# Prompt attention of a hybrid decoder step: new places in the written-out order for the next head's transposes, the values' low part, the page sums and the maxima

## The chip, the cores and the metric

One Trainium2 chip, one of its cores. The kernel runs as one program on that core; the time is the device time of one execution in microseconds (us), the median of several runs.

## The reference

The whole kernel is one inference step of a hybrid decoder layer: a joint input projection, three token mixers, gates and an output projection. The change touches one stage, the forgetting attention over the prompt (2048 positions, 8 heads of 64), and a side calculation that shares its engines. Cut to what matters:

```python
def fox_attention(q, k, v, fq, fk, q_pos, k_pos):       # fq, fk: cumulated log forget values
    s = einsum('bqhd,bkhd->bhqk', q, k) * dh ** -0.5
    s = s + fq[..., :, None] - fk[..., None, :]
    s = where(k_pos <= q_pos, s, -inf)                   # causal
    return einsum('bhqk,bkhd->bqhd', softmax(s), v)

logf_all = concatenate([cache_logf[page_table], logf])   # sample group: 8 sequences x 8192 positions
cum_f = cumsum(logf_all, axis=1)
```

## The kernel before

Four stages run one after another: `project`, `attend_prompt`, `attend_sample` and the output. Barriers part them. Within a stage each engine has its own instruction stream, in an order fixed in the source, and streams meet at semaphores only.

`attend_prompt` works head by head. The 16 key tiles and 16 query tiles of 128 positions are cut into 4 groups of queries (`g`, 512 columns each); group g meets 4(g+1) key tiles (`j`). So a head has 4+8+12+16 = 40 steps, written (g, j) here, and the stage has 320. Products are made with float32r operands in two parts (high and low), so the scores take two matmuls of 512 columns (`kA`/`qA` hold the high part and the extra rows with decays and maxima, `kB`/`qB` the low parts and a second copy) and the weighing of the values takes three (`v_hi`·`p_hi`, `v_lo`·`p_hi`, `v_hi`·`p_lo`). The steps of the diagonal blocks are 512, 384, 256 and 128 columns wide.

The order is the function `all_steps`, which every engine walks through with its own class. For step s:

- `score(s)`: two matmuls on PE into one of 2 buffers `st_ps`; ACT takes the exponential into `probs` (L1429) and then casts the probabilities of step s-1 to `p_hi` (L1405).
- `past`: in every second head (a "pair"), sums over the cached log forget values for the later sample stage. DVE scans at (1, 0..7), PE has one small matmul at (2, 2), DVE makes `rest` at (2, 4) and three 128x1024 tensor operations (L1507, L1509, L1512) at (2, 5), (2, 6), (2, 7). GpSimd (POOL) gathers the values with an indirect DMA at (0, 0) and waits there until it has landed (L1373).
- `maximum`: row maxima that the softmax subtracts, one group ahead: PE multiplies `kA` and `qA` into one of 2 buffers `max_ps` (L1598), DVE reduces them (L1518). `negate` joins them (L1526), and `turn_max` brings them into row form: four PE transposes (L1583), one ACT copy into `qA` (L1423). `turn_max` is the last thing in the last step of a group, behind `weigh`.
- `split(h+1)` at (1, 4): DVE casts the next head's values to `v_hi` (L1455), POOL subtracts to get `v_lo` (L1378) for all 16 tiles.
- `decay(h+1)` at (2, 7), `turn(h+1, c)`: the next head's keys are transposed at (2, 8), (2, 9), (2, 10), (2, 11), its queries at (3, 1), (3, 3), (3, 5), (3, 7): four PE transposes each (L1571), then an ACT copy to `kA`/`qA` (L1416, L1418), then two DVE operations of 64x512 to `kB`/`qB` (L1475 and L1476, L1479 and L1480). Each turn of PE waits for the DVE part of the turn before, since they share a PSUM buffer.
- `weigh(s-4)`: POOL subtracts `p_lo` = `probs` - `p_hi` (L1392), PE has the three matmuls (L1635 to L1637). P is held in rings of 6.
- `turn_back`, 6 steps behind the last step of a group, that is at (1, 1), (1, 5), (2, 5), (3, 5): ACT copies the finished output out of PSUM (L1440), PE transposes it back (L1644), DVE normalizes it.

Before the first step, head 0 does all of its eight turns, its first maxima and `turn_max(0, 0)`. DVE clears the unused rows of `kA`, `qA` (`pad`, L1448) for head 0 there and for head 1 at (0, 0) and (0, 1) of head 0, and those of `o_sb` at (0, 2).

SP stores the page sums of a pair and loads heads 4 to 7, with waits on `turned`, `max_turned`, `vlo_ready` and `past_step`; after the last pair's page sums it starts the first loads of the sample stage.

Of the kernel before, what the change touches and what calls it, by code (L numbers as in the profile page):

```python
# [27 lines left out]
F32 = mybir.dt.float32  # L28
# [4 lines left out]
P = 128  # L33
# [1089 lines left out]
def attend_prompt(nc, arena, z, y_a, cache_logf, cache_k, page_table, decay_past):  # L1123
# [21 lines left out]
    LAG, BACK = 4, 2  # L1145
    P_RING = 6
    TURNS = 2 * GROUPS
    IN_GROUP = P // N_PAGES
    with ExitStack() as stack:
# [34 lines left out]
        consts, padded, filled = m.sem("consts"), m.sem("padded"), m.sem("filled")  # L1184
# [20 lines left out]
        FIRST_CONSTS, CONSTS = 4, 13  # L1205
# [21 lines left out]
        def all_steps(do):  # L1227

            do.split(0)
            do.decay(0)  # L1230
            for c in range(TURNS):
                do.turn(0, c)
# [4 lines left out]
            ends = {}  # L1237
            for s in range(STEPS + LAG + BACK):
                h, n = divmod(s, N_FIN)
                if s < STEPS:  # L1240
                    g, j = FIN[n]
                    last = h == HEADS - 1
                    do.score(s)
                    if h % 2 == 0:
                        do.past(h // 2, g, j)
# [7 lines left out]
                    if not last:  # L1253
                        if g == 1 and j == 4:
                            do.split(h + 1)
                        if g == 2 and j == 7:
                            do.decay(h + 1)
                        if g == 2 and j >= 8:
                            do.turn(h + 1, j - 8)
                        if g == 3 and j < 8 and j % 2 == 1:  # L1260
                            do.turn(h + 1, GROUPS + j // 2)
                        if g == 3 and 9 <= j < 9 + QG:
                            do.maximum(h + 1, MAX_UNITS[0][j - 9])
                            if j == 8 + QG:
                                do.negate(h + 1, 0)
                if LAG <= s < STEPS + LAG:
                    do.weigh(s - LAG)
                if s < STEPS:
                    if j == QG * (g + 1) - 1 and (g < GROUPS - 1 or not last):
                        do.turn_max(*((h, g + 1) if g < GROUPS - 1 else (h + 1, 0)))  # L1270
                done = s - LAG - BACK
                if done >= 0 and done % N_FIN + 1 in FIN_END:
                    do.turn_back(done // N_FIN, FIN_END.index(done % N_FIN + 1))

        class Part:

            past = decay = turn = turn_max = maximum = negate = score = weigh = turn_back = split = lambda self, *where: None

        @block.sync
        def _(sp):  # L1280
# [6 lines left out]
            def load(h):  # L1287
                if h >= 4:
                    sp.wait_ge(turned, (h - 1) * TURNS)
                    sp.wait_ge(max_turned, (h - 1) * GROUPS)  # L1290
                    sp.wait_ge(vlo_ready, h - 1)
# [9 lines left out]
            def begin_sample():  # L1301
# [4 lines left out]
                sp.wait_ge(vlo_ready, 2)  # L1306
# [34 lines left out]
        def _(pool):  # L1341
            def ones_of(k, q, done):
# [5 lines left out]
            ones_of(arena.k_first, arena.q_first, consts)  # L1348
            pool.memset(v_hi[:, :, :, HEAD_DIM:HEAD_DIM + 1].bitcast(F32), 1.0).then_inc(consts, 1)
# [18 lines left out]
            def gather(group):  # L1368
                pool.wait_ge(past_stored, 16)
                wait_from(pool, past_step, 3 * group)  # L1370
                pool.indirect_dma_start(lf[:], None, cache_logf.rearrange("l n k h -> (l n) (k h)"),
                                        bass.IndirectOffsetOnAxis(ap=page_of[:, group:group + 1], axis=0)).then_inc(gathered, 16)
                pool.wait_ge(gathered, 16 * (group + 1))  # L1373

            class GpSimdPart(Part):
                def split(self, h):
                    pool.wait_ge(vhi_ready, h + 1)
                    pool.tensor_tensor(v_lo[:, h % 2], v_of(h), v_hi[:, h % 2, :, 0:HEAD_DIM].bitcast(F32),  # L1378
                                       ALU.subtract).then_inc(vlo_ready, 1)
                    if h == 0:  # L1380
# [17 lines left out]
        def _(act):  # L1398
# [8 lines left out]
            class ScalarPart(Part):  # L1407
                def turn(self, h, c):
                    hh, at = h % 2, slice((c % GROUPS) * BLK, (c % GROUPS + 1) * BLK)
                    bank = c % 2 if h == 0 else 0  # L1410
                    if c == 0:
                        act.wait_ge(padded, 2 * min(h + 1, 2))
                        wait_from(act, st_done, (h - 1) * N_FIN)
                    act.wait_ge(turned, h * TURNS + (c + 1))
                    if c < GROUPS:
                        act.copy(kA[0:AUG, hh, at], t_ps[0:AUG, bank, :]).then_inc(k_high, 1)  # L1416
                    else:
                        act.mul(qA[0:AUG, hh, at], t_ps[0:AUG, bank, :], HEAD_DIM ** -0.5).then_inc(q_high, 1)  # L1418
# [16 lines left out]
                def turn_back(self, h, g):  # L1435
                    n = h * GROUPS + g
                    act.wait_ge(pv_done, h * N_FIN + FIN_END[g])
                    act.wait_ge(padded, 5)
# [6 lines left out]
        def _(dve):  # L1445

            def pad(x, hh):
                dve.memset(x[HEAD_DIM:P, hh].bitcast(F32), 0.0).then_inc(padded, 1)  # L1448

            class VectorPart(Part):  # L1450
                def split(self, h):
                    dve.wait_ge(v_loaded[slot_of(h)], loads_of(h))
                    wait_from(dve, pv_done, (h - 1) * N_FIN)
                    wait_from(dve, vlo_ready, h - 1)
                    dve.tensor_copy(v_hi[:, h % 2, :, 0:HEAD_DIM], v_of(h)).then_inc(vhi_ready, 1)  # L1455

                def decay(self, h):
# [4 lines left out]
                    if h == 0:  # L1462
                        pad(kA, 0)
                        pad(qA, 0)

                def turn(self, h, c):
                    hh, at = h % 2, slice((c % GROUPS) * BLK, (c % GROUPS + 1) * BLK)
                    bank = c % 2 if h == 0 else 0
                    if c == 0:
                        wait_from(dve, st_done, (h - 1) * N_FIN)  # L1470
                    dve.wait_ge(turned, h * TURNS + (c + 1))
                    src = t_ps[0:HEAD_DIM, bank, :]
                    if c < GROUPS:
                        dve.wait_ge(k_high, h * GROUPS + (c + 1))
                        dve.tensor_copy(kB[HEAD_DIM:P, hh, at], src)  # L1475
                        dve.tensor_tensor(kB[0:HEAD_DIM, hh, at], src, kA[0:HEAD_DIM, hh, at].bitcast(F32), ALU.subtract).then_inc(k_low, 1)  # L1476
                    else:
                        dve.wait_ge(q_high, h * GROUPS + (c - GROUPS + 1))
# [1259 lines left out]
```

## Time and profile before

| | |
|---|---|
| median of 3 runs | 3863.25 us (3862.15 to 3867.77) |
| the profiled execution: its time, its span | 3863.69 us, 3861.9 us |
| PE, DVE, ACT, POOL busy over the span | 94%, 48%, 47%, 37% |
| first and last score matmul of `attend_prompt` | 1815.2 us, 2466.7 us |
| granted TensorE clock over the span | 0.978 |

Matmuls are pipelined: a 512-column matmul is shown as some 0.4 us, while the next one starts 0.23 us after it. So the busy share of PE says little, and the waits and the start-to-start times say more. A wait is idle time after the modelled end of the matmul before it.

### The profile page before, as it was taken

To read this page: it belongs to the slowest core of one execution; us is meant where nothing else is said; L and a number is where in the kernel's file an instruction comes from. 1 tells how busy PE (TensorE), PEld (TensorE's weight loads), DVE (VectorE), ACT (ScalarE), POOL (GpSimd) and SP (SyncE) were. 2 spreads that over 40 slices of the span, in tenths; PEclk is the share of its full clock that TensorE was granted. 3 is DMA by queue.
4 is the path that set the end of the run, shared out by engine and by line. 5 is a ranking of instruction groups with operands and counts; after the bars stand their busy time and mean duration, and the time that the engine had idled before them with its cause. 6 is when DMAs were issued, how large, how long until landed. Compare 5 with 4: busy or idle time off the path is not lost. (4 is left out here: it accounts for less than half of the span.)

```text
span 3861.9 us, 54053 instructions
## 1 busy us (share of the span) xinstructions
PE 3622.5 (94%) x17931; PEld 2838.3 (73%) x17931; DVE 1861.5 (48%) x3114; ACT 1807.4 (47%) x3704; POOL 1414.2 (37%) x1063
## 2 busy tenths in 40 slices
PE   8999999999999999997787787899999999799999
PEld 7788888787788888885555555577777777588787
DVE  3234432323134533333545545488888888644432
ACT  4224433445224533442555565677777777411222
POOL 0011232220011232211555565577777777422200
PEclk9999999999999999997999999999999999899999
DMA  4234343333233344324001212299999999654422
GB/s 160 85 108 137 115 146 124 107 137 121 89 124 113 119 143 141 123 94 107 12 17 28 53 25 69 84 340 334 334 331 334 331 329 336 223 171 154 151 89 79
DMA packets 378554, 590.38 MB, mean 153 GB/s; under 512 B 93381, under 2 KB 114485, under 8 KB 378298
## 3 DMA queue, kind: packets, MB, share of 16 engines
q1 hardware_dynamic: 366146, 579.94, 44.4%
q10 hardware_dynamic: 11584, 5.13, 0.5%
q8 instruction: 145, 2.38, 0.3%
q0 software_dynamic: 576, 2.10, 0.2%
q14 instruction: 103, 0.84, 0.1%
HBM read 475.25 MB, written 111.83 MB: 152 GB/s over the span
## 5 line engine op out<-in xcount | busy, mean ns | idle before, releaser
L996 PE MATMUL prj_z_ps<-prj_w_hi,prj_h_hi 128*128 128x512 f32 x2312 | 923.9, 400 | 2.7 <-DVE prj_w_lo L792 2.7
L998 PE MATMUL prj_z_ps<-prj_w_hi,prj_h_lo 128*128 128x512 f32 x2312 | 902.4, 390 | 0.0
L997 PE MATMUL prj_z_ps<-prj_w_lo,prj_h_hi 128*128 128x512 f32 x2312 | 901.0, 390 | 0.0
L1874 POOL TENSOR_TENSOR sa_v_lo<-sa_v_raw,sa_v_hi 128x1024 fp32r<-128x1024 f32 x256 | 609.1, 2401 | 215.6 <-DVE sa_v_hi L2013 215.2
L998 PEld LDWEIGHTS prj_z_ps<-prj_w_hi,prj_h_lo 128*128 128x128 f32 x2312 | 434.2, 188 | 93.7
L996 PEld LDWEIGHTS prj_z_ps<-prj_w_hi,prj_h_hi 128*128 128x128 f32 x2312 | 435.3, 188 | 89.7 <-DVE prj_w_lo L792 5.4
L997 PEld LDWEIGHTS prj_z_ps<-prj_w_lo,prj_h_hi 128*128 128x128 f32 x2312 | 435.4, 188 | 84.7
L1392 POOL TENSOR_TENSOR pa_p_lo<-pa_probs,pa_p_hi 128x512 fp32r<-128x512 f32 (+1 forms) x320 | 362.0, 1147 | 230.0 <-ACT pa_p_hi L1405 207.0
L2007 DVE TENSOR_TENSOR sa_kT_lo<-sa_t_ps,sa_kT_hi 128x512 fp32r<-128x512 f32 x512 | 345.3, 686 | 136.3 <-ACT sa_kT_hi L1896 132.8
L424 POOL TENSOR_TENSOR prj_dist<-prj_cum 128x256 f32<-128x256 f32 x132 | 88.6, 671 | 796.3 <-DVE prj_cum L863 796.3
L1896 ACT CAST sa_kT_hi<-sa_t_ps 128x512 fp32r<-128x512 f32 x512 | 291.6, 590 | 125.5 <-PE sa_t_ps L2160 118.8
L2160 PE MATMUL sa_t_ps<-arena_ident,arena_k_raw 128*128 128x128 f32 x2048 | 300.9, 277 | 26.0 <-DVE sa_kT_lo L2007 18.1
L2160 PEld LDWEIGHTS sa_t_ps<-arena_ident,arena_k_raw 128*128 128x128 f32 x2048 | 241.8, 141 | 105.3 <-DVE sa_kT_lo L2007 33.2
L792 DVE TENSOR_TENSOR prj_w_lo<-arena_w_raw,prj_w_hi 128x512 fp32r<-128x512 f32 x274 | 193.2, 749 | 204.7 <-ACT prj_w_hi L660 203.8
L675 ACT ACTIVATE prj_z_sb<-prj_z_ps 128x512 f32<-128x512 f32 x153 | 91.2, 596 | 406.8 <-PE prj_z_ps L998 406.5
L1429 ACT ACTIVATE pa_probs<-pa_st_ps 128x512 f32<-128x512 f32 (+1 forms) x320 | 171.0, 534 | 227.7 <-PE pa_st_ps L1620 137.7
L672 ACT COPY prj_z_sb<-prj_z_ps 128x512 f32<-128x512 f32 (+2 forms) x124 | 72.2, 582 | 428.7 <-PE prj_z_ps L998 417.7
L1518 DVE TENSOR_REDUCE pa_part_max<-pa_max_ps 128x1 f32<-128x512 f32 (+2 forms) x320 | 183.4, 606 | 182.4 <-PE pa_max_ps L1598 145.3
L432 POOL TENSOR_TENSOR prj_kE<-prj_kT,prj_dec 128x256 f32<-128x256 f32 x115 | 93.0, 808 | 404.1 <-ACT prj_dec L711 385.1
L2223 PE MATMUL sa_o_ps<-sa_v_hi,sa_p_both 128*128 128x512 f32 x512 | 215.3, 420 | 8.4 <-POOL sa_v_lo L1874 5.3
L2166 PE MATMUL sa_s_ps<-sa_kT_hi,sa_q_both 128*128 128x512 f32 x512 | 212.6, 415 | 0.0
L2224 PE MATMUL sa_o_ps<-sa_v_lo,sa_p_both 128*64 128x512 f32 x512 | 204.0, 399 | 0.0
(327 smaller groups left out, 6447.2 us busy)
## 6 DMA issues: line engine op xcount, KB each, us to landing
arena_k_raw<-in_cache_k_dram SPq DMA_DIRECT2D x512, 256.0 KB, 4.0
sa_v_raw<-in_cache_v_dram SPq DMA_DIRECT2D x512, 256.0 KB, 4.3
arena_w_raw<-in_w_main_dram SPq DMA_DIRECT2D x272, 256.0 KB, 4.1
z_scratch<-prj_z_sb SPq DMA_DIRECT2D x272, 256.0 KB
arena_mg<-z_scratch SPq DMA_DIRECT2D x51, 512.0 KB, 4.2
arena_cu<-extp_scratch SPq DMA_DIRECT2D x48, 256.0 KB
arena_x_in<-in_x_all_dram SPq DMA_DIRECT2D x17, 512.0 KB, 3.7
prj_aux<-z_scratch SPq DMA_DIRECT2D x34, 256.0 KB, 2.8
```

The lines of the kernel that those rows point to most:

```text
L792: dve.tensor_tensor(w_lo[:, s % W_RING, 0:columns(s)], w_raw[:, s % RAW, 0:columns(s)], w_hi[:, s % W_RING, 0:columns(s)].bitcast(F32), AL ...
L996: pe.matmul(out, h_hi[:, slot_of(t), k], hi, start=(k == 0), stop=False)
L997: pe.matmul(out, h_hi[:, slot_of(t), k], lo, start=False, stop=False)
L998: mm = pe.matmul(out, h_lo[:, slot_of(t), k], hi, start=False, stop=(k == KC - 1))
L1392: pool.tensor_tensor(p_lo[:, s % P_RING, 0:w], probs[:, s % P_RING, 0:w], p_hi[:, s % P_RING, 0:w].bitcast(F32), ALU.subtract).then_inc(pl ...
L1874: pool.tensor_tensor(v_lo[:, w % 2, at], v_raw[:, w % RING, at], v_hi[:, w % 2, at].bitcast(F32), ALU.subtract).then_inc(vlo_ready, 1)
L1896: act.copy(kT_hi[:, g % 2, :, j * PAGE:(j + 1) * PAGE], heads_of(t_ps[:, j % 2])).then_inc(khi_ready, 1)
L2007: dve.tensor_tensor(kT_lo[:, g % 2, :, at], heads_of(t_ps[:, j % 2]), kT_hi[:, g % 2, :, at].bitcast(F32), ALU.subtract).then_inc(klo_read ...
L2160: mm = pe.transpose(t_ps[:, j % 2, pair * PAGE:(pair + 1) * PAGE], k_raw[:, g % RING, j, pair * P:(pair + 1) * P], ident[:])
L2166: pe.matmul(out, q, hi(pair), start=(pair == 0), stop=False, skip_group_check=True)
L2223: pe.matmul(out, p_both[:, slot, j], v_hi[:, slot, j], start=begin, stop=False, skip_group_check=True)
L2224: mm = pe.matmul(out[0:R], p_both[:, slot, j, 0:R], v_lo[:, slot, j], start=False, stop=end, skip_group_check=True)
```

## The change

The steps stay; what moves is where the side work stands in the order, with the semaphores split to suit.

- The next head's turns go key, query, key, query (`TURN_ORDER`), at (2, 4), (2, 6), (2, 8), (2, 10), (3, 0), (3, 2), (3, 4), (3, 6). `decay` goes to (2, 3).
- `turn_max` of a group stands ahead of `weigh`, at (0, 3), (1, 7), (2, 10), (3, 14).
- POOL's `v_lo` is made in two halves, at (2, 0) and (2, 2); the DVE cast stays at (1, 4).
- ACT's copy of a finished output (`take`) is one step earlier than the transposes.
- POOL no longer waits for the gather to land, it waits for the one before it at the next gather.
- The three page-sum operations of DVE go to (3, 9), (3, 11), (3, 13).
- Head 0 does four turns (groups 0 and 1) before its first step and the other four in (0, 0) to (0, 3); in its turns ACT writes the second copy for `kB`/`qB` (`first_b`), DVE only the low part. POOL clears `qA` for head 0; head 1's clearing goes to (2, 0) and (2, 2) of head 0, that of `o_sb` to (0, 3).

```diff
-    LAG, BACK = 4, 2
+    LAG, TAKE, BACK = 4, 1, 2
+    TURN_ORDER = [x for c in range(GROUPS) for x in ((0, c), (1, c))]
+    TURN_AT = {(2, 4): 0, (2, 6): 1, (2, 8): 2, (2, 10): 3, (3, 0): 4, (3, 2): 5, (3, 4): 6, (3, 6): 7}
+    MAX_TURN_AT = {(0, 3): 1, (1, 7): 2, (2, 10): 3, (3, 14): 0}
...
             do.split(0)
+            do.split_low(0, 0)
+            do.split_low(0, 1)
             do.decay(0)
-            for c in range(TURNS):
-                do.turn(0, c)
+            for n in range(4):
+                do.turn(0, n)
...
                     do.score(s)
+                    if h == 0 and g == 0:
+                        do.turn(0, 4 + j)
                     if h % 2 == 0:
                         do.past(h // 2, g, j)
...
-                        if g == 1 and j == 4:
+                        if (g, j) == (1, 4):
                             do.split(h + 1)
-                        if g == 2 and j == 7:
+                        if g == 2 and j in (0, 2):
+                            do.split_low(h + 1, j // 2)
+                        if (g, j) == (2, 3):
                             do.decay(h + 1)
-                        if g == 2 and j >= 8:
-                            do.turn(h + 1, j - 8)
-                        if g == 3 and j < 8 and j % 2 == 1:
-                            do.turn(h + 1, GROUPS + j // 2)
-                        if g == 3 and 9 <= j < 9 + QG:
-                            do.maximum(h + 1, MAX_UNITS[0][j - 9])
-                            if j == 8 + QG:
+                        if (g, j) in TURN_AT:
+                            do.turn(h + 1, TURN_AT[g, j])
+                        if g == 3 and 8 <= j < 8 + QG:
+                            do.maximum(h + 1, MAX_UNITS[0][j - 8])
+                            if j == 7 + QG:
                                 do.negate(h + 1, 0)
+                    if (g, j) in MAX_TURN_AT and (g < GROUPS - 1 or not last):
+                        do.turn_max(h if g < GROUPS - 1 else h + 1, MAX_TURN_AT[g, j])
                 if LAG <= s < STEPS + LAG:
                     do.weigh(s - LAG)
-                if s < STEPS:
-                    if j == QG * (g + 1) - 1 and (g < GROUPS - 1 or not last):
-                        do.turn_max(*((h, g + 1) if g < GROUPS - 1 else (h + 1, 0)))
-                done = s - LAG - BACK
-                if done >= 0 and done % N_FIN + 1 in FIN_END:
-                    do.turn_back(done // N_FIN, FIN_END.index(done % N_FIN + 1))
+                for do_it, done in ((do.take, s - LAG - TAKE), (do.turn_back, s - LAG - BACK)):
+                    if 0 <= done < STEPS and done % N_FIN + 1 in FIN_END:
+                        do_it(done // N_FIN, FIN_END.index(done % N_FIN + 1))
...
@@ gpsimd
+            pool.wait_ge(consts, FIRST_CONSTS)
+            pad(qA, 0)
+            pool.wait_ge(q_padded, 1)
...
                 wait_from(pool, past_step, 3 * group)
+                wait_from(pool, gathered, 16 * group)
                 pool.indirect_dma_start(lf[:], None, cache_logf.rearrange("l n k h -> (l n) (k h)"),
...
-                pool.wait_ge(gathered, 16 * (group + 1))
...
+                def split_low(self, h, half):
+                    tiles = slice(half * T // 2, (half + 1) * T // 2)
+                    if half == 0:
+                        pool.wait_ge(vhi_ready, h + 1)
...
@@ scalar, turn
                     act.wait_ge(turned, h * TURNS + (n + 1))
+                    if h == 0:
+                        act.mul((kB, qB)[is_q][B_HIGH[is_q], hh, at], t_ps[0:HEAD_DIM, bank, :],
+                                (1.0, HEAD_DIM ** -0.5)[is_q]).then_inc(first_b, 1)
...
@@ vector, past
-                    if j == 5:
+                    if (g, j) == (3, 9):
                         dve.wait_ge(rest_ready, pair + 1)
                         dve.tensor_tensor(log_rest, wide, cum[:], ALU.subtract).then_inc(past_step, 1)
-                    if j == 6:
+                    if (g, j) == (3, 11):
                         dve.tensor_tensor(d_hi[:], wide, cum[:], ALU.subtract).then_inc(past_step, 1)
-                    if j == 7:
+                    if (g, j) == (3, 13):
...
@@ tensor, score
-                        pe.wait_ge(k_low, (h + 1) * GROUPS)
-                        pe.wait_ge(q_low, (h + 1) * GROUPS)
+                        pe.wait_ge(q_low, h * GROUPS + (g + 1))
+                        if h == 0:
+                            pe.wait_ge(first_b, 2 * (g + 1))
+                    if j % QG == 0:
+                        pe.wait_ge(k_low, h * GROUPS + (j // QG + 1))
```

## Rows read from the trace of the kernel before

**Rows 1.** The page, part 1: busy us, share of the span, instructions.

```profile
PE 3622.5 (94%) x17931; PEld 2838.3 (73%) x17931; DVE 1861.5 (48%) x3114; ACT 1807.4 (47%) x3704; POOL 1414.2 (37%) x1063
```

**Rows 2.** Waits, 1815 to 2475 us: waiter, awaited, total us, times, longest.

```profile
POOL pa_p_lo L1392 <- DMA pa_lf<-in_cache_logf_dram,pa_page_of: 11.1, 3, 4.2
PE pa_o_ps L1635 <- POOL pa_p_lo L1392: 38.1, 11, 5.0
PE pa_t_ps L1571 <- DVE pa_kB L1476: 24.6, 21, 1.2
PE pa_st_ps L1615 <- ACT pa_qA L1423: 21.3, 32, 0.7
PE pa_o_ps L1644 <- ACT pa_o_sb L1440: 13.7, 25, 1.0
PE pa_t_ps L1571 <- DVE pa_qB L1480: 8.7, 14, 0.9
```

**Rows 3.** Windows: groups 0, 2 of heads 3, 4; group 2 of head 7.

```profile
2071.20:2080.05 8.85, 6.72 (x41) 4.52 (x41) 4.61 (x9) 3.71 (x9) 3.76 (x5) 1.00 0.01 2
2101.00:2127.30 26.30, 20.55 (x109) 14.32 (x109) 16.25 (x28) 15.37 (x30) 13.75 (x12) 1.00 0.00 1
2151.36:2162.43 11.07, 8.41 (x40) 5.29 (x40) 5.07 (x10) 3.71 (x9) 6.47 (x7) 0.85 0.09 37
2184.93:2213.03 28.10, 21.57 (x110) 14.44 (x110) 19.55 (x32) 15.37 (x30) 15.91 (x12) 1.00 0.00 1
...
2429.20:2448.36 19.16, 17.93 (x93) 12.20 (x93) 10.28 (x19) 13.05 (x26) 13.15 (x12) 1.00 0.05 15
```

**Rows 4.** Windows: steps (1, 4) and (1, 5) of heads 3, 4 and 7.

```profile
2087.05:2097.72 10.67, 5.83 (x26) 3.33 (x24) 4.12 (x8) 3.10 (x7) 7.73 (x6) 0.84 0.00 0
2169.60:2181.36 11.76, 6.75 (x26) 4.02 (x24) 4.75 (x10) 2.94 (x6) 8.40 (x6) 0.74 0.24 69
2421.25:2425.87 4.62, 4.34 (x25) 2.51 (x24) 3.60 (x7) 3.10 (x7) 4.05 (x4) 1.00 0.00 0
```

**Rows 5.** Timeline of POOL, heads 4 and 7: start, us, instruction, idle before.

```profile
2172.64 2.24 POOL L1378 TENSOR_TENSOR pa_v_lo<-pa_v_raw,pa_v_hi 128x1024 fp32r<-128x1024 f32 x1 [8.12 <-DVE pa_v_hi L1455]
...
2192.87 1.29 POOL L1392 TENSOR_TENSOR pa_p_lo<-pa_probs,pa_p_hi 128x512 fp32r<-128x512 f32 x1 [0.19 <-PE pa_o_ps L1637]
...
2197.28 4.18 POOL L1392 TENSOR_TENSOR pa_p_lo<-pa_probs,pa_p_hi 128x512 fp32r<-128x512 f32 x2 [0.89 <-ACT pa_p_hi L1405]
...
2430.79 0.46 POOL L1392 TENSOR_TENSOR pa_p_lo<-pa_probs,pa_p_hi 128x128 fp32r<-128x128 f32 x1 [1.77 <-ACT pa_p_hi L1405]
```

**Rows 6.** Timeline of PE where group 3 of head 3 ends.

```profile
2149.87 0.39 PE L1637 MATMUL pa_o_ps<-pa_p_lo,pa_v_hi 128*65 128x512 f32 x1
2150.09 0.60 PE L1583 MATMUL pa_t_ps<-arena_ident,pa_q_aug 128*67 128x128 f32 x4
2151.36 0.50 PE L1615 MATMUL pa_st_ps<-pa_qA,pa_kA 128*128 128x512 f32 x1 [0.67 <-ACT pa_qA L1423]
```

**Rows 7.** Timeline of PE: two turns of keys, (2, 9) and (2, 10), head 4.

```profile
2204.96 0.65 PE L1571 MATMUL pa_t_ps<-arena_ident,pa_k_aug 128*67 128x128 f32 x4 [1.15 <-DVE pa_kB L1476]
...
2207.77 0.65 PE L1571 MATMUL pa_t_ps<-arena_ident,pa_k_aug 128*67 128x128 f32 x4 [1.16 <-DVE pa_kB L1476]
```

**Rows 8.** Timeline of DVE, head 4, steps (2, 6) and (2, 7).

```profile
2196.77 1.22 DVE L1509 TENSOR_TENSOR pa_d_hi<-pa_rest,pa_cum 128x1024 fp32r<-128x1024 f32 x1
2197.91 1.28 DVE L1518 TENSOR_REDUCE pa_part_max<-pa_max_ps 128x1 f32<-128x512 f32 x2
```

**Rows 9.** Windows: before the first step; group 0 of head 0.

```profile
1791.40:1815.20 23.80, 12.24 (x44) 8.23 (x44) 19.15 (x26) 6.46 (x10) 6.46 (x19) 0.50 0.73 155
1815.20:1828.18 12.98, 8.92 (x28) 5.67 (x28) 8.36 (x13) 3.52 (x8) 2.99 (x3) 0.50 0.00 0
```

**Rows 10.** Timeline of DVE before the first step: a clearing, a turn's copy.

```profile
1793.18 1.76 DVE L1448 MEMSET pa_kA<- 64x2048 f32 x1 [0.48 <-issue]
...
1799.22 0.69 DVE L1475 CAST pa_kB<-pa_t_ps 64x512 fp32r<-64x512 f32 x1
```

More of the change, by code:

```diff
@@ L1341, in _, with pad @@
         def _(pool):
+            def pad(x, hh):
+                pool.memset(x[HEAD_DIM:P, hh].bitcast(F32), 0.0).then_inc(q_padded, 1)
             def ones_of(k, q, done):
@@ L1407, in _, with turn @@
             class ScalarPart(Part):
[L1408 to L1412, printed above, removed]
-                        wait_from(act, st_done, (h - 1) * N_FIN)
-                    act.wait_ge(turned, h * TURNS + (c + 1))
-                    if c < GROUPS:
+                def turn(self, h, n):
+                    is_q, c = TURN_ORDER[n]
+                    hh, at = h % 2, slice(c * BLK, (c + 1) * BLK)
+                    bank = n % 2 if h == 0 else 0
+                    if n == 0:
+                        wait_from(act, st_done, (h - 1) * N_FIN)
+                    act.wait_ge(turned, h * TURNS + (n + 1))
+                    if h == 0:
+                        act.mul((kB, qB)[is_q][B_HIGH[is_q], hh, at], t_ps[0:HEAD_DIM, bank, :],
+                                (1.0, HEAD_DIM ** -0.5)[is_q]).then_inc(first_b, 1)
+                    if not is_q:
+                        act.wait_ge(k_padded, min(h + 1, 2))
                         act.copy(kA[0:AUG, hh, at], t_ps[0:AUG, bank, :]).then_inc(k_high, 1)
                     else:
+                        act.wait_ge(q_padded, min(h + 1, 2))
                         act.mul(qA[0:AUG, hh, at], t_ps[0:AUG, bank, :], HEAD_DIM ** -0.5).then_inc(q_high, 1)
@@ L1433, in score, with take @@
                         high(s)
-                def turn_back(self, h, g):
+                def take(self, h, g):
                     n = h * GROUPS + g
                     act.wait_ge(pv_done, h * N_FIN + FIN_END[g])
-                    act.wait_ge(padded, 5)
+                    act.wait_ge(o_padded, 1)
                     wait_from(act, o_back, n - 1)
@@ L1462, in decay, with turn @@
                     if h == 0:
[L1463 to L1469, printed above, removed]
+                        pad(kA, 0, k_padded)
+                def turn(self, h, n):
+                    is_q, c = TURN_ORDER[n]
+                    hh, at = h % 2, slice(c * BLK, (c + 1) * BLK)
+                    bank = n % 2 if h == 0 else 0
+                    if n == 0:
@@ L1481, in turn @@
                                                  in1=qA[0:HEAD_DIM, hh, at].bitcast(F32), op0=ALU.mult, op1=ALU.subtract).then_inc(q_low, 1)
                 def past(self, pair, g, j):
-                    if pair == 0 and g == 0 and j < 3:
-                        if j < 2:
-                            pad((kA, qA)[j], 1)
+                    if pair == 0 and (g, j) == (0, 3):
+                        dve.memset(o_sb[HEAD_DIM:P], 0.0).then_inc(o_padded, 1)
+                    if pair == 0 and (g, j) in ((2, 0), (2, 2)):
+                        if j == 0:
+                            pad(kA, 1, k_padded)
@@ L1551, in past, with turn @@
                         pe.matmul(t_ps[:, 1, 0:HEADS], later[:], whole[:], start=True, stop=True).then_inc(later_summed, 1)
-                def turn(self, h, c):
-                    bank = c % 2 if h == 0 else 0
-                    if c == 0:
-                        pe.wait_ge(consts, FIRST_CONSTS)
-                        if h >= 2:
-                            pe.wait_ge(filled, 4)
+                def turn(self, h, n):
+                    is_q, c = TURN_ORDER[n]
+                    bank = n % 2 if h == 0 else 0
+                    if h >= 2 and n == 0:
+                        pe.wait_ge(filled, 4)
+                    if n == 0:
+                        pe.wait_ge(consts, 1)
                         pe.wait_ge(k_loaded[slot_of(h)], loads_of(h))
@@ L1577, in turn_max @@
                     if h == 0 and g == 0:
+                        pe.wait_ge(q_low, 2)
+                        pe.wait_ge(first_b, 4)
+                    if h == 0 and g == 1:
                         pe.wait_ge(q_low, GROUPS)
+                        pe.wait_ge(first_b, TURNS)
                     wait_from(pe, max_set, h * GROUPS + g)
```

81 lines of the change are left out of this document (44 added, 37 removed).

## The prediction

> **What bounds the kernel now.** First the page: over the span PE is busy 94%, every other engine under half [rows 1]. That is an average over four stages, and the change touches one, `attend_prompt`, so everything is read between 1815 and 2475 us. The stages run one after another behind barriers, so what this stage saves the whole saves, as long as its loads are not late.
>
> Second the waits of PE there [rows 2]. The reader is to see that no engine is full: PE, in order, stops for others at fixed places of each head. POOL's `p_lo` costs it 38.1 us, the DVE part of turns 24.6 + 8.7, ACT's copy of maxima 21.3 (0.67 us in each of 32 groups), ACT's copy of a finished output 13.7. A wait is counted from the modelled end of the transposes, so each costs about 0.25 us more than shown: the matmul before starts at 2149.87, the four transposes at 2150.09, they issue in about 0.35, and the score starts at 2151.36 [rows 6], so 0.92 us is lost, not 0.67.
>
> Third the windows, which price the places. Head 7 has no next head, so it is a built-in control: its group 2 takes 19.16 us against 26.30 and 28.10 in heads 3 and 4 [rows 3], and its steps (1, 4) and (1, 5) take 4.62 against 10.67 and 11.76 [rows 4]. All sums below are against the profiled execution (3863.69 us, span 3861.9 us), 0.4 us above the median of the runs.
>
> **The change part by part.**
>
> *Low part of the values.* At (1, 4) POOL stands in front of `p_lo`, waiting 8.12 us for the DVE cast, which is queued behind this step's reductions, and then works 2.24 us [rows 5]. PE then stops 5.0 us [rows 2], and its clock falls (0.84 and 0.74 in these windows, that is partly at 1.2 GHz, against 1.00 in head 7) [rows 4]. The two steps lose 6.05 and 7.14 us, mean 6.6, in each of 7 heads: 46 us. In the new order POOL comes to `v_lo` some six steps after the cast. The cast stays, about 0.7 us of DVE that is busy 3.60 of 4.62 us there [rows 4]; I charge half: -2.5. The halves, 1.1 us each (half of 2.24), go in front of the `p_lo` of (1, 4) and (1, 6), beside narrow steps: in head 7 POOL idles 1.77 us before a single one of these [rows 5], and four steps lie between a score and its weighing. I take them at nothing; with that cover gone they cost 7 x 2.2 = 15 us. Term: 43, between 28 and 46.
>
> *Gather.* Behind it POOL waits 11.1 us for the DMA in three even heads [rows 2], and head 4's group 0 takes 11.07 against 8.85 us in head 3 [rows 3]. I put the three heads' loss at 9.5 (2.2 in head 4, the other two waits being longer) and leave 1.5 for issuing the DMA, which stays. DVE needs the data a whole group later. Term: 8, between 5 and 11.
>
> *Maxima turned sooner.* At (2, 10) and (3, 14) a whole step lies between the transposes and the score that needs them, so the 0.92 us goes: 8 + 7 places, 13.8 us. At (1, 7) only `weigh` (three matmuls at 0.22 or 0.23, 0.69 us) comes between, and ACT's exponential and cast stand before its copy: I take half, 8 x 0.45. At (0, 3) PE waits for the last reductions anyway: nothing. Term: 17, between 10 and 18.
>
> *Output copy a step sooner.* 13.7 us shown in 25 waits [rows 2], plus what the model hides, about 0.17 each in 31: 19. The copy itself then stands in ACT's queue in a step in which ACT is not full (15.37 of 26.30 us in a group 2 [rows 3]). Term: 17, between 10 and 19.
>
> *Turns every second step.* A key turn comes 2.81 us after the last [rows 7]: that is its chain, PE to ACT to DVE and back. Before, the keys' four stand in four steps in a row, each shorter than that, so PE waits in each; the queries' are two steps apart and wait less (8.7 us in all [rows 2]). New, from PE's own work (score 0.47, maxima 0.5, weigh 0.69, turn 0.35, turn-back 0.41): (2, 4)+(2, 5) 4.1 us, (2, 6)+(2, 7) 3.7, both over 2.81; (2, 8)+(2, 9) 2.55 and (2, 10)+(2, 11) 2.4, so waits of 0.3 and 0.4. But DVE now has, over (2, 4) to (2, 7), eight reductions at 0.64 to 0.69 [rows 8], two turns at 1.4 and a turn-back at 0.6, some 8.7 us against 7.8 of PE: 0.9 more. Group 2 of head 7 without its two waits (0.92, 0.6) is 17.6; with four turns (1.4) and 1.6 of waits it is 20.6. Heads 3 and 4 have a mean of 27.2 [rows 3]: gain 6.6, of which 1.5 is already booked in the two parts above, leaves 5.1 x 7 = 36. In group 3 the waits only change places: (3, 0)+(3, 1) 0.3, (3, 2)+(3, 3) about 1.0, against 1.75 now. What is queued behind a turn in DVE is the next step's reductions, and PE's maxima wait for those. Bounds: at the bottom, the turn's wait for ACT holds DVE through each of (2, 4) to (2, 7), about 3 us more a head; at the top no wait at all. Term: 36, between 15 and 46.
>
> *Page sums in the last group.* The three DVE operations leave a place where DVE was full; that gain (28.10 against 26.30) is in the mean above. At their new places DVE has nothing but four reductions. But POOL paces here: beside them its `p_lo` took 4.18 us for two against 1.29 for one [rows 5, 8], so 1.6 us more, and some 0.6 more beside the first. POOL has one to two steps of lead, so PE loses perhaps 0.7 in each of 4 heads: -3, between -9 and 0. The Trainium skill ("SBUF — State Buffer", section "Who interferes with whom") says that a DVE instruction with two SBUF inputs and a GpSimd one that reads SBUF shut each other out for the whole instruction. This case's trace agrees in kind (4.18 for two). By the rule the three operations would hold POOL up 4.5 us a pair; in place of my -3 the sum would have about -11.
> SP's stores of the page sums come some 30 us later and behind them load(5), load(7) and the first loads of the sample stage. load(5) and load(7) wait for the following head anyway; the last has all of head 7 as cover. Nothing.
>
> *Start.* DVE is busy 19.15 of the 23.8 us before the first step [rows 9]: eight turns of two operations at 0.69 are 11.0, two clearings of 1.76 are 3.5 [rows 10]. New, it has one clearing and four single operations, 10.0 us less; a turn now has two ACT copies in its chain, so I take 9.5. POOL's clearing is not in the trace: from 0.2 us for 128 columns, 0.2 to 3.4 us; either is over before the first query turn needs it. Group 0 of head 0 took 12.98 us, with 4.4 us of clearing, against 8.85 for a head without [rows 3, 9]. Now each of its four steps has a turn whose chain (ACT has two copies) stands in DVE's queue before the reductions: 8.85 + 4 x 2.6 = 19.3, so -6.5. Two clearings in (2, 0) and (2, 2), where reductions nearly fill DVE: -2.5. Term: 0, between -8 and +7.
>
> Sum: 43 + 8 + 17 + 17 + 36 - 3 + 0 = 118; 3863.7 - 118 = 3746 us. Group 1 then has some 13.6 us and group 3 some 22, so a middle head 8.9 + 13.6 + 20.6 + 22 = 65, against (2466.7 - 1815.2) / 8 = 81 now.
>
> **The rivals.**
>
> *A: DVE takes PE's place.* Each turn in (2, 4) to (2, 7) waits in DVE's queue for ACT, the reductions behind it are late, the next score with them, and head 0's group 0 does the same. For it: DVE was busy 19.55 of 28.10 us in head 4's group 2 [rows 3] and the turns' 2.7 us fall where the reductions are. Against it: PE's step is longer there too. Then the turns give 15 to 20 rather than 36, copies and maxima 26 rather than 34, start -6: sum about 84, 3780 us.
>
> *B: the waits go entirely.* The chains overlap better, the start gains 5, no POOL loss: about 144, 3720 us.
>
> *C: POOL's queue again (the other side).* One mechanism: whatever stands in front of a `p_lo` in POOL's queue makes PE wait as the old `v_lo` did, and lets the clock fall. There are now 14 halves, 3 gathers and 12 page-sum operations, 29 places. At 6.6 us each that is 191 us against a gain of 118: 3937 us; it decides for slower from 118/29 = 4.1 us a place. Against it: in the old place POOL waited 8 us in front, here only 1 us of work stands.
>
> *D: the change does only the part at (1, 4) and the gather*, since PE's time between the waits is set by ACT and POOL rates: 45 to 60 gained, 3805 to 3815 us. Against it: head 7 runs group 2, without turns, in 19.16 us [rows 3].
>
> **How the numbers follow.** Forecast 0.62, its own range 3728 to 3766. A 0.20, B 0.10, D 0.05, C 0.03. The range, 3716 to 3788, takes in A and B and leaves out C, D and the tails. Within 0.2% (8 us, about what a measurement of this kernel tells from no change) only something between D and C could land: 0.01. Faster 0.96, slower 0.03.
>
> **What would show it.** Waits of PE: `p_lo` from 38.1 to under 6; L1615 on L1423 from 21.3 to about 9; L1644 on L1440 to about 1; turns from 33 to some 8; reductions (DVE) up. Windows: (1, 4)+(1, 5) of a middle head under 5.5 us, group 2 20 to 21, group 3 about 22, clock 1.00 throughout; group 0 of head 0 about 19. The first score near 1806, the last near 2349. The prediction is wrong if group 2 stays above 23, if group 3 of even heads is 2 us above odd ones, or if group 0 of head 0 is over 22.

## The result and the profile after

The changed kernel takes 3747.28 us (median; 3743.07 to 3749.07) against 3864.05 us before on the same chips: ratio 0.9695, 95% interval 0.9678 to 0.9712. It is faster by 117 us; forecast were 118 us less and 3746 us.

The page, part 1, as in [rows 1]:

```profile
PE 3585.3 (96%) x17931; PEld 2823.4 (75%) x17931; DVE 1867.7 (50%) x3105; ACT 1810.5 (48%) x3712; POOL 1423.5 (38%) x1072
```

Work is the same to within about a per cent on each engine; what went is waiting, and with it time at the lower clock (granted 0.978 over the span before, 0.988 now). The waits of PE between 1805 and 2355 us, with the columns of [rows 2] (L1673 was L1635, L1653 was L1615, L1602 was L1571, L1682 was L1644, L1633 was L1598, L1618 was L1583):

```profile
PE pa_max_ps L1633 <- DVE pa_part_max L1545: 16.4, 26, 2.1
PE pa_t_ps L1602 <- DVE pa_kB L1500: 6.0, 14, 0.6
PE pa_t_ps L1602 <- DVE pa_qB L1505: 5.3, 7, 0.8
PE pa_o_ps L1673 <- POOL pa_p_lo L1408: 5.1, 9, 0.9
PE pa_st_ps L1653 <- ACT pa_qA L1444: 4.7, 9, 0.7
PE pa_t_ps L1602 <- DVE pa_k_aug L1481: 4.7, 6, 0.8
PE pa_t_ps L1618 <- DVE pa_q_aug L1553: 4.6, 6, 0.8
...
PE pa_o_ps L1682 <- ACT pa_o_sb L1461: 0.7, 1, 0.7
```

POOL's share fell from 38.1 to 5.1 us, the turns' from 33.3 to 11.3 (with the wait of a first turn for `decay`, `k_aug` above, from 40.5 to 16.0), the maxima's copy from 21.3 to 4.7, the output copy's from 13.7 to 0.7. In front of the four transposes of `turn_max`, one step earlier now, PE waits more than before, 7.8 us against 5.1 in all. The reductions of DVE now head the list, with 16.4 us against 10.3.

Windows of the changed kernel: group 0 of head 3, then groups 2 and 3 of head 3, then the same of head 4 (compare [rows 3]); last, steps (1, 4) and (1, 5) of heads 3 and 4 (compare [rows 4]).

```profile
2021.88:2030.76 8.88, 6.56 (x41) 4.51 (x39) 4.61 (x9) 3.71 (x9) 5.49 (x7) 1.00 0.00 0
2043.95:2065.40 21.45, 19.91 (x108) 14.15 (x109) 16.37 (x28) 15.14 (x30) 15.14 (x14) 1.00 0.01 2
2065.40:2087.50 22.10, 21.07 (x117) 14.84 (x116) 8.43 (x16) 19.25 (x39) 17.88 (x16) 1.00 0.37 71
2087.51:2096.38 8.87, 6.56 (x41) 4.50 (x39) 4.97 (x10) 3.83 (x10) 6.10 (x7) 1.00 0.21 60
2110.70:2132.58 21.88, 20.23 (x110) 14.38 (x111) 17.67 (x31) 15.12 (x30) 14.98 (x14) 1.00 0.01 3
2132.58:2156.43 23.85, 21.62 (x117) 15.07 (x116) 12.64 (x19) 19.38 (x39) 20.12 (x15) 1.00 0.45 110
...
2037.00:2041.20 4.20, 4.13 (x25) 2.61 (x24) 4.09 (x6) 3.06 (x6) 3.43 (x4) 1.00 0.00 0
2103.15:2107.95 4.80, 4.30 (x26) 2.70 (x24) 4.80 (x10) 2.59 (x5) 3.74 (x4) 1.00 0.52 147
```

The reader is to see three things. Group 0 of an even head now costs what an odd one's does (8.87 us in head 4, where it was 11.07). The two steps of the old split fell from 10.67 and 11.76 to 4.20 and 4.80, and the granted clock there is 1.00, where it was 0.84 and 0.74. And group 3 of an even head is 1.75 us longer than that of an odd one (23.85, 22.10), which it was not in the kernel before (heads 3 and 4):

```profile
2127.28:2151.36 24.08, 21.67 (x117) 14.82 (x117) 8.50 (x16) 19.30 (x38) 16.68 (x14) 1.00 0.37 71
2213.03:2237.07 24.04, 21.63 (x117) 14.82 (x117) 8.51 (x16) 19.41 (x38) 18.32 (x16) 1.00 0.43 110
```

### The profile page after: what moved, and what is told of

It is laid out like the page before. It is cut to its first block and busy times, and to the rows that moved or that the text cites. A ratio compares the mean times of both kernels' runs of the same rounds, so it can differ in the third digit from the quotient of the medians.

```text
span 3747.3 us, 54477 instructions
## 1 busy us (share of the span) xinstructions
PE 3585.3 (96%) x17931; PEld 2823.4 (75%) x17931; DVE 1867.7 (50%) x3105; ACT 1810.5 (48%) x3712; POOL 1423.5 (38%) x1072
## 3 DMA queue, kind: packets, MB, share of 16 engines
q8 instruction: 146, 2.39, 0.3%
```

## The experiments

Whole runs of this kernel scatter by several us, so each run is read twice: by its time, and by the length of the stage in its profile, from the first to the last score matmul. Both numbers stand ahead of the semicolon of the row for the first score matmul among the instructions of `st_ps` (shortest, median, longest in ns, then first and last start in us). In the kernel before:

```profile
L1615 PE MATMUL pa_st_ps<-pa_qA,pa_kA x320: 220/393/796, 1815.2 to 2466.7; 128*128 128x512 f32 x128, 128*128 128x256 f32 x32
```

In the changed kernel:

```profile
L1653 PE MATMUL pa_st_ps<-pa_qA,pa_kA x320: 220/393/796, 1805.5 to 2348.6; 128*128 128x512 f32 x128, 128*128 128x256 f32 x32
```

The same row of every other kernel is in the table. The stage scatters too: groups 0 and 1 of head 0 took 34.3 us in the changed kernel's profile and 32.9 to 33.9 in six kernels whose edits lie elsewhere, so a difference of a us or so says nothing by itself. Where an effect is that small, the lengths of the groups that it touches decide.

| kernel | time, us | ratio to before (95%) | first to last score, us | stage, us | against the changed kernel's |
|---|---|---|---|---|---|
| before | 3864.05 | | 1815.2 to 2466.7 | 651.5 | +108.4 |
| changed | 3747.28 | 0.9695 (0.9678 to 0.9712) | 1805.5 to 2348.6 | 543.1 | |
| low part back | 3792.08 | 0.9808 (0.9792 to 0.9825) | 1806.9 to 2394.6 | 587.7 | +44.6 |
| low part alone, on the kernel before | 3819.94 | 0.9886 (0.9869 to 0.9902) | 1816.0 to 2424.0 | 608.0 | 43.5 under before |
| turns back | 3774.13 | 0.9763 (0.9747 to 0.9779) | 1806.2 to 2371.9 | 565.7 | +22.6 |
| gather wait back | 3755.76 | 0.9722 (0.9705 to 0.9738) | 1805.2 to 2357.5 | 552.3 | +9.2 |
| output copy back | 3768.52 | 0.9754 (0.9737 to 0.9770) | 1807.7 to 2373.0 | 565.3 | +22.2 |
| turn_max back | 3765.47 | 0.9752 (0.9735 to 0.9768) | 1806.8 to 2367.1 | 560.3 | +17.2 |
| eight turns first | 3746.80 | 0.9694 (0.9678 to 0.9711) | 1813.2 to 2348.8 | 535.6 | -7.5 |
| page sums back | 3751.96 | 0.9706 (0.9690 to 0.9722) | 1804.7 to 2351.8 | 547.1 | +4.0 |
| page sums with one input | 3740.67 | 0.9677 (0.9661 to 0.9694) | 1807.1 to 2342.8 | 535.7 | -7.4 |
| page sums between turns | 3740.53 | 0.9683 (0.9667 to 0.9700) | 1805.8 to 2340.6 | 534.8 | -8.3 |
| decay early | 3742.17 | 0.9688 (0.9672 to 0.9704) | 1809.3 to 2345.6 | 536.3 | -6.8 |
| all moved on | 3738.05 | 0.9675 (0.9659 to 0.9691) | 1806.1 to 2338.9 | 532.8 | -10.3 |

The intervals of the last four rows overlap each other's and the changed kernel's. By time alone these four are not shown to be faster than it.

### The low part of the values, undone and alone

```diff
                         if (g, j) == (1, 4):
                             do.split(h + 1)
-                        if g == 2 and j in (0, 2):
-                            do.split_low(h + 1, j // 2)
+                            do.split_low(h + 1, 0)
+                            do.split_low(h + 1, 1)
```

> The changed kernel with both halves of v_lo made at (1, 4) again, behind the DVE cast. Theory (the term of the prediction, 43 us): POOL waits about 8 us in front, PE about 5 us in each of 7 heads, the clock falls there; steps (1, 4) and (1, 5) together take 10.5 to 11.8 us instead of 4.2 to 4.8, the kernel about 3790 us (3783 to 3796). Rival: with the other waits gone, POOL's lead now covers a good part and the time is under 3770 us.

Measured: 3792 us, the stage 44.6 us longer. POOL's timeline in head 4 of this kernel:

```profile
2131.93 2.39 POOL L1394 TENSOR_TENSOR pa_v_lo<-pa_v_raw,pa_v_hi 128x512 fp32r<-128x512 f32 x2 [7.39 <-DVE pa_v_hi L1476]
```

Its windows of (1, 4) and (1, 5), heads 3 and 4 (compare [rows 4]):

```profile
2055.30:2067.10 11.80, 6.74 (x26) 4.03 (x24) 4.29 (x8) 3.05 (x6) 8.45 (x7) 0.73 0.01 1
2128.90:2140.00 11.10, 5.94 (x25) 3.45 (x24) 4.74 (x10) 2.85 (x6) 8.06 (x7) 0.69 0.26 72
```

The halves themselves are not the cost (2.39 us for both); it is that they stand where POOL must wait 7.39 us for the cast, and the clock in these two steps is 0.73 and 0.69 again. Then the part alone, on the kernel before:

> The kernel before with one part of the change alone: v_lo in halves at (2, 0) and (2, 2). Theory (the parts add up, and undoing this part in the changed kernel cost 45 us): about 3820 us (3816 to 3826), steps (1, 4) and (1, 5) together 5 us in odd heads. Rival (in the old order the halves meet other waits of POOL and PE, so the part is worth less alone): 3832 us or more.

Measured: 3820 us, the stage 43.5 us shorter than before. So this part adds up: 43.5 alone, 44.6 undone, 43 in the prediction. Steps (2, 0) to (2, 3) of heads 0, 4 and 6, where the halves now stand, take 6.04 to 6.05 us against 6.05 to 6.07 before. Two things hold the 43.5 down. At (1, 5) PE now waits 0.27 to 0.28 us in seven heads for the output copy, a wait that the long one at (1, 4) had covered. And step (2, 11), with a wait of PE of 1.0 to 1.2 us in it and in each of the three steps before it, takes 5.5 us at a granted clock of 0.69 in heads 0, 1 and 6 and 4.1 us in heads 2 to 5 (1.00 in heads 4 and 5). In the kernel before only two heads, 1 and 5, have the 5.5 us.

### The turns

```diff
-    TURN_AT = {(2, 4): 0, (2, 6): 1, (2, 8): 2, (2, 10): 3, (3, 0): 4, (3, 2): 5, (3, 4): 6, (3, 6): 7}
+    TURN_AT = {(2, 8): 0, (2, 9): 1, (2, 10): 2, (2, 11): 3, (3, 1): 4, (3, 3): 5, (3, 5): 6, (3, 7): 7}
+    LATER_ORDER = [(q, c) for q in (0, 1) for c in range(GROUPS)]     # heads 1 to 7
...
-                        if (g, j) == (2, 3):
+                        if (g, j) == (2, 7):
                             do.decay(h + 1)
```

> The changed kernel with the turns of heads 1 to 7 and the decays at their old places and in their old order (four keys in (2, 8) to (2, 11), four queries in (3, 1) to (3, 7)); head 0 as in the changed kernel. Theory (term of 36 us, the page sums' old place booked in it): about 3778 us, group 2 of odd heads from 21.4 to 25.5 or 26, group 3 unchanged within 0.5. Rival (DVE takes PE's place in group 2 of the changed kernel, so the move was worth half): under 3765 us, group 2 under 24.

Measured: 3774 us and a stage 22.6 us longer, between the two theories: 3.1 us a head in group 2 where four were expected.

### Gather, output copy, maxima

```diff
+                pool.wait_ge(gathered, 16 * (group + 1))        # gather wait back
...
-    LAG, TAKE, BACK = 4, 1, 2                                  # output copy back
+    LAG, TAKE, BACK = 4, 2, 2
...
-    MAX_TURN_AT = {(0, 3): 1, (1, 7): 2, (2, 10): 3, (3, 14): 0}   # turn_max back: and behind weigh
+    MAX_TURN_AT = {(0, 3): 1, (1, 7): 2, (2, 11): 3, (3, 15): 0}
```

> The changed kernel with POOL waiting for the gather to land again. Theory (term of 8 us): group 0 of heads 2, 4, 6 from 8.88 us back to 11 to 12.7, the kernel 3755 us (3752 to 3757). Rival (with turn_max a step earlier there is less cover, so it costs more): group 0 of these heads above 13 us, 3760 us or more.

Measured: 3756 us, stage +9.2. Group 0 of heads 2, 4 and 6 takes 12.3 to 12.5 us, 10.6 more in all, as the theory has it.

> The changed kernel with ACT's copy of a finished output in the same step as the transposes. Theory (term of 17 us): PE waits about 0.5 to 0.9 us at (1, 1), (1, 5), (2, 5), (3, 5), the kernel about 3763 us (3758 to 3766). Rival (in the changed kernel DVE or the turns' chain sets the pace around these steps, so most of it is hidden): under 3755 us.

Measured: 3769 us, stage +22.2, above the range that either theory gave. PE waits 0.60 us at (1, 1), 0.28 at (1, 5), 0.50 at (2, 5) and 0.98 at (3, 5).

> The changed kernel with turn_max behind weigh in the last step of a group, as before. Theory (term of 17 us: 0.92 at (2, 11) and (3, 15), 0.45 at (1, 7)): L1653 waits 0.67 us in all 32 groups, the kernel about 3763 us (3758 to 3766). Rival (the reductions of group 0 follow the first score anyway, and the score's delay is filled by them): under 3755 us.

Measured: 3765 us, stage +17.2.

### The start

```diff
-            for n in range(4):
+            for n in range(TURNS):
                 do.turn(0, n)
...
-                    if h == 0 and g == 0:
-                        do.turn(0, 4 + j)
```

> The changed kernel with all eight turns of head 0 ahead of its first step. Theory (the start's term is near 0, what is saved before the first step is paid in group 0): first score 6 to 7 us later, group 0 of head 0 from 18.1 to 10 or 11 us, the kernel within 3 us of 3747. Rival (the early first step was the gain, the waits in group 0 come from the slow clock of this stretch): slower by 5 us or more.

Measured: 3746.8 us against 3747.3. The first score comes 7.7 us later and the stage is 7.5 us shorter: moving four turns behind the first step is worth nothing here. The other parts of the start (the clearings, ACT's second copy) were not undone one by one.

### The page sums

```diff
-                    if (g, j) == (3, 9):        # page sums back: (2, 5), (2, 6), (2, 7)
+                    if (g, j) == (2, 5):
...
-                        dve.tensor_tensor(log_rest, wide, cum[:], ALU.subtract)     # one input
+                        dve.tensor_reduce(rest[:], cum[:], AX.X, ALU.max)
...
-                    if (g, j) == (3, 9):        # between turns: (2, 9), (2, 11), (3, 1)
+                    if (g, j) == (2, 9):
```

(The second edit is made at all three operations; `d_hi` is cleared once instead.)

> The changed kernel with the three page-sum operations of DVE back at (2, 5), (2, 6), (2, 7). Theory (POOL is held up wherever they stand, and DVE is full in group 2): group 3 of heads 0, 2, 4, 6 falls from 23.9 to about 22.1, their group 2 rises from 21.9 by 2 to 3 us, the total changes by less than 5 us either way. Rival 1 (the move was the gain it was meant to be): slower by 8 us or more. Rival 2 (it only costs POOL's lead in group 3): faster by 5 us or more.

Measured: 3752 us, stage +4.0. Group 3 of heads 0, 2, 4, 6 fell to 22.1 us, group 2 rose by 3.0. So the move was worth 4 to 5 us, with 12 gained and 7 given back.

> The changed kernel with the three DVE operations of the page sums at (3, 9), (3, 11), (3, 13), each with two SBUF inputs, replaced by reductions of the same 128x1024 tile with one SBUF input (the page sums themselves are left out). Theory (POOL's subtraction is held up by a DVE operation with two SBUF inputs): a p_lo of 512 columns stays at 1.3 us or less beside them, PE no longer waits for p_lo in (3, 12) and (3, 13), group 3 of even heads takes 22.1 to 22.4 us instead of 23.9, the kernel 3740 us. Rival (DVE's own queue is the reason: maxima and normalization behind these operations are late): group 3 of even heads stays above 23.3 us.

Measured: 3741 us, stage -7.4, group 3 of even heads 22.13 to 22.20 us. The timeline of POOL, DVE and PE in head 4 of the changed kernel, where the first of the three operations starts and where PE waits; ahead of it, POOL's six subtractions there (shortest, median, longest in ns):

```profile
L1408 POOL TENSOR_TENSOR pa_p_lo<-pa_probs,pa_p_hi x6: 1293/1769/2282, 2145.2 to 2154.3; 128x512 fp32r<-128x512 f32 x6
...
2145.15 10.47 POOL L1408 TENSOR_TENSOR pa_p_lo<-pa_probs,pa_p_hi 128x512 fp32r<-128x512 f32 x6 [0.29 <-ACT pa_p_hi L1421]
...
2145.71 1.82 DVE L1534 TENSOR_TENSOR pa_lf<-pa_rest,pa_cum 128x1024 f32<-128x1024 f32 x1
...
2150.95 0.44 PE L1673 MATMUL pa_o_ps<-pa_p_hi,pa_v_hi 128*65 128x512 f32 x1 [0.34 <-POOL pa_p_lo L1408]
...
2153.16 0.45 PE L1673 MATMUL pa_o_ps<-pa_p_hi,pa_v_hi 128*65 128x512 f32 x1 [0.88 <-POOL pa_p_lo L1408]
```

The same place in this kernel, POOL and DVE:

```profile
2142.76 6.45 POOL L1410 TENSOR_TENSOR pa_p_lo<-pa_probs,pa_p_hi 128x512 fp32r<-128x512 f32 x5 [0.29 <-ACT pa_p_hi L1423]
...
2143.31 1.21 DVE L1536 TENSOR_REDUCE pa_rest<-pa_cum 128x8 f32<-128x1024 f32 x1
```

Six subtractions of POOL take 10.47 us: the three that begin while one of the three DVE operations with two SBUF inputs runs take 2.24 to 2.28 us each, the other three 1.29. So POOL is held up by 2.9 us. Beside reductions that read the same tile and last 1.21 us, each subtraction takes 1.29 (6.45 for five). DVE's load is nearly the same, so its own queue is not the reason. The DVE operations are held up too, by less: they take 1.82, 1.32 and 1.51 us there.

> The changed kernel with the three page-sum operations of DVE at (2, 9), (2, 11) and (3, 1), the steps between turns, where p_lo is narrow. Theory (POOL is held up by them only where its columns are full, and DVE has room after the eight reductions of group 2): group 3 of even heads falls from 23.9 to about 22.2 and group 2 rises by less than 1 us: 3742 to 3745 us. Rival (they stand in front of the turns' DVE part, so the turn chain grows by up to the 2.1 us of the first): even heads' group 2 and 3 together above 45.8 us, no gain.

Measured: 3740.5 us, stage -8.3, group 3 of even heads 22.1, group 2 unchanged at 21.9. POOL is held up here as well, by 3.4 us: a subtraction of 512 columns takes 2.72 us, one of 256 takes 1.72 (0.73 elsewhere), one of 512 takes 2.24. But the narrow tiles of 384, 256 and 128 columns lie between them, POOL is idle again for 0.71 us before the last, and PE does not wait for it. The first of them, and the DVE operation beside it (head 4):

```profile
2124.88 2.72 POOL L1408 TENSOR_TENSOR pa_p_lo<-pa_probs,pa_p_hi 128x512 fp32r<-128x512 f32 x1 [0.16 <-ACT pa_p_hi L1421]
...
2125.24 1.21 DVE L1534 TENSOR_TENSOR pa_lf<-pa_rest,pa_cum 128x1024 f32<-128x1024 f32 x1
```

### Decay, and all of it moved on

```diff
-                        if (g, j) == (2, 3):
+                        if (g, j) == (2, 1):
                             do.decay(h + 1)
```

> The changed kernel with decay at (2, 1) instead of (2, 3). Theory (PE's wait in front of the first turn at (2, 4) is for this small DVE copy, queued behind two reductions): step (2, 4) of heads 1 to 6 from 3.08 to about 2.1 us, head 0 unchanged, 6 us in all, 3741 us. Rival (reductions that the copy holds up at (2, 1) cost the same there): no change.

Measured: 3742 us, stage -6.8: group 2 of heads 1 to 6 is 0.9 to 1.0 us shorter, 5.7 in all; the rest of the 6.8 is head 0's scatter. The size is the theory's, the reason is not. The copy is not only queued behind reductions, it is itself long. DVE and POOL in head 3 of the changed kernel, then of this one:

```profile
2050.31 1.29 DVE L1481 COPY pa_k_aug<-arena_decay 128x32 f32<-128x32 f32 x1
2050.28 1.28 POOL L1408 TENSOR_TENSOR pa_p_lo<-pa_probs,pa_p_hi 128x512 fp32r<-128x512 f32 x1
...
2048.07 0.18 DVE L1481 COPY pa_k_aug<-arena_decay 128x32 f32<-128x32 f32 x1
2048.21 1.30 POOL L1408 TENSOR_TENSOR pa_p_lo<-pa_probs,pa_p_hi 128x512 fp32r<-128x512 f32 x1 [0.97 <-ACT pa_p_hi L1421]
```

In heads 1 to 6 of the changed kernel the copy begins just after a subtraction of POOL, lasts 1.26 to 1.29 us and ends 0.04 to 0.05 us behind it. At (2, 1) it begins 0.14 us before POOL's and lasts 0.18. It was too long by 1.1 us, and PE waited 0.8 for it, so behind the reductions alone it would have cost nothing. The gain comes from not meeting POOL, and that is luck of the new place, since the theory had not looked for it.

```diff
-    TURN_AT = {(2, 4): 0, (2, 6): 1, (2, 8): 2, (2, 10): 3, (3, 0): 4, (3, 2): 5, (3, 4): 6, (3, 6): 7}
+    TURN_AT = {(2, 4): 0, (2, 6): 1, (2, 8): 2, (2, 11): 3, (3, 1): 4, (3, 4): 5, (3, 6): 6, (3, 8): 7}
-                    if (g, j) == (3, 9):        # and (3, 11), (3, 13)
+                    if (g, j) == (2, 9):        # and (2, 10), (3, 0)
-                    if pair == 0 and (g, j) in ((2, 0), (2, 2)):
+                    if pair == 0 and (g, j) in ((1, 6), (1, 7)):
```

> The changed kernel with what the runs point to: page sums at (2, 9), (2, 10), (3, 0), decay at (2, 1), the clearings for head 1 at (1, 6) and (1, 7) of head 0, turns at (2, 4), (2, 6), (2, 8), (2, 11), (3, 1), (3, 4), (3, 6), (3, 8). Theory, by waits seen in the changed kernel: 8 us for the page sums, 6 for decay, 2.5 for the clearings, 0.85 x 7 for the turn at (2, 10) and 1.5 x 7 for those at (3, 2) and (3, 4): 33 us, about 3714 us (3708 to 3724). Rival (with its waits gone PE meets ACT's and POOL's rates in group 3, or the turn at (3, 8) runs into the maxima): 3728 us or more.

Measured: 3738 us, the lowest median of all kernels, but 24 us short of the theory, and its stage of 532.8 us is only 2.0 and 3.5 us below that of two of its parts alone. The turn moved from (2, 10) to (2, 11) gave what it was to give: group 2 of odd heads takes 19.70 us, 0.83 below that with `decay` early alone. The expectation failed in three places. The clearings side by side cost group 2 of head 0 1.5 us more, not 2.5 less: PE waits 3.4 us at (2, 1), where it waited 1.2 there and 1.0 at (2, 3). Page sums at (2, 10) and (3, 0) without a step between made PE wait 1.0 us for `p_lo` at (3, 0) of even heads. And the turns' new places took the waits out of the list but not the time out of group 3: 22.25 us against 22.10 in odd heads. The trace shows part of it at (3, 4), where the weight load waits and no matmul is charged (`PEld`, head 3):

```profile
2066.45 0.41 PEld L1602 LDWEIGHTS pa_t_ps<-arena_ident,pa_q_aug 128*67 128x67 f32 x4 [0.55 <-DVE pa_kB L1500]
...
2068.99 0.42 PEld L1682 LDWEIGHTS pa_o_ps<-arena_ident,pa_o_sb 128*128 128x128 f32 x4 [0.54 <-ACT pa_o_sb L1461]
```

Step (3, 5) has the same work in both kernels, and no wait of a matmul in either; with the weight load's wait it takes 1.78 us (head 3) in place of 1.51. Where the rest of group 3's time went is open.

The two moves that worked singly (page sums between turns, 6.9 us in group 3 of even heads; decay early, 5.7) were not run together without the rest; by their parts that kernel's stage would be some 530 us, below this one, which is an estimate.

## Why the prediction was right, point by point

The undone parts add up to 44.6 + 22.6 + 9.2 + 22.2 + 17.2 + 4.0 = 119.8 us. The stage is 108.4 us shorter and begins 9.7 us earlier, 118.1 together. By the medians the undone parts add up to 124 us and the kernel is 117 us faster; by the ratios, each to the kernel before in the same runs, it is 129 against 118. So the parts overlap by some 2 to 12 us, and each term is known to a few us, no better.

- *Low part, 43.* Right in size and mechanism: 44.6 undone, 43.5 alone. The halves cost nothing at (2, 0) and (2, 2), as taken; the kernel with this part alone shows it.
- *Gather, 8.* Right: 9.2 by the stage, 10.6 by group 0 of the three heads.
- *Maxima sooner, 17.* Right: 17.2. PE still waits 0.5 us at (1, 0), as expected of the place (0, 3). At (1, 7), where half was taken, the wait for the copy is gone (4.7 us left in all, about 9 forecast).
- *Output copy, 17.* Mis-sized: 22.2, above the upper bound of 19. Undone, the copy made PE wait 0.98 us at (3, 5), where I had priced each of 31 at about 0.6. The waits shown in the kernel before undercounted it, because at (3, 5) a turn's wait (0.3 us) stood just in front and took part of the time: head 7, which has no turn there, waited 0.95 us. That is 3.4 us in seven heads. The other part is (1, 5): the copy undone makes PE wait 0.28 us there in each of 8 heads, 2.3 us. The kernel before showed no such wait, since PE had just stopped 5 us for `p_lo` at (1, 4); with the low part moved it comes out, there as in the kernel with that part alone. Together that is the 5 us: the term was priced from the waits shown, and two of its four places were covered by other waits.
- *Turns, 36, with the page sums' old place in it; page sums, -3.* The mechanism was right, both sizes off. Turns alone measure 22.6, the page sums' move 4.0, together 27 against 33. The step that was mis-sized is the sum for the new group 2, which left `decay` out: at (2, 4) the first turn of heads 1 to 6 waits 0.8 us for it, because this DVE copy of 0.18 us begins while POOL subtracts and takes 1.26 to 1.29. It stood in front of (2, 8) before, where PE waited 1.0 us for it, and was moved along with the turn. So group 2 of an odd head takes 21.45 us, where I had 20.6; with `decay` moved alone it takes 20.53, and group 2 of the six heads is 5.7 us shorter, which is about the 6 us that are missing. The waits of the turns themselves came near: 0.6 us at (2, 10) and none at (3, 0), where I had 0.3 and 0.4; 0.3 and 0.8 at (3, 2) and (3, 4), where I had 0.3 and 1.0.
- *Page sums at the new place.* I had -3 and named "2 us above odd ones" as a sign of error: 1.75 us in each of four heads, 7 us, within the bounds of -9 to 0. The Trainium skill ("SBUF — State Buffer", section "Who interferes with whom") says that a DVE instruction with two SBUF inputs contends with a GpSimd one that reads SBUF, and that a reduction never does. The runs agree with both: 2.24 to 2.28 us for a subtraction beside the one, 1.29 beside the other. The 4.5 us a pair that the prediction worked out by the rule did not come: POOL was held up by 2.9 us, and PE lost 1.75 of them, since POOL had lead.
- *Start, 0.* Right, and for the four turns shown by the run with eight turns first. First score at 1805.5 (forecast near 1806), group 0 of head 0 18.15 us (19.3), clearings 2.6 us (2.5; steps (2, 0) to (2, 3) of head 0 against head 4).
- *The rivals.* A as a whole is excluded by the time (3780) and by copies and maxima, 39 us where it had 26. But part of it came: the turns' 22.6 lies nearer its 15 to 20 than 36, and PE's waits for reductions rose from 10.3 to 16.4 us. B and D are excluded by the time, C by the time and by the list of waits: nothing in front of a `p_lo` costs PE more than 0.9 us. That the total came within 2 us is luck: the output copy was 5 us under, turns and page sums 6 us over.

The rest of the program took 1395.2 us from the last score to the end before and 1398.7 after; over the experiments this stretch lies between 1394 and 1402 us with no edit in it. That alone makes single times scatter by several us.

## What to carry to other kernels

When several in-order engines feed each other, look for what stands in front of a wait in each queue, not for how long it works: 2.2 us of POOL work cost 6.4 us a head because it waited behind DVE, and nothing once the cast stood four steps or more ahead. A unit that skips the work in question, here the last head, prices its removal from one trace. A wait shown is a lower bound where another stands just in front of it: remove the first, and the second comes out, as the output copy's did at (1, 5). When a step is moved, look at its small helpers (here `decay`) in the trace, at their length too and not only at their place in the queue. And give DVE operations with two SBUF inputs a place where POOL has room, here among the narrow tiles.

## What the runs showed of the hardware that was not expected

A DVE `tensor_tensor` of 128x1024 with both inputs in SBUF lasted 1.20 to 2.12 us, and its length alone does not tell whether it met POOL. In the changed kernel it took 1.82 us and POOL's next subtraction 2.28 in place of 1.29; between turns it took 1.21 and POOL's subtraction 2.72. The engine that pays can be either, or both.

Small DVE copies pay as well. The `decay` copy of 128x32 took 0.18 us where it began with no subtraction of POOL running, and otherwise ended 0.04 to 0.05 us behind POOL's subtraction: it lasted 0.86 us in three heads of the kernel before and 1.26 to 1.29 in six of the changed one. The page sums' scans of 128x128 take 0.40 us at best; 16 of 32 took 0.67 to 1.37 us in the changed kernel, against 1 of 32 (0.80 us) before. What these cost PE was not isolated.

And a wait at a weight load can cost PE time that no list of the matmul's waits shows, some 0.27 us at (3, 5) above: taking the shown waits out of group 3 left its length where it was.
